# FOX squares summed over heads in two one-pass products of their high and low parts

## What is computed

```python
def rmsnorm(x, g):
    y = xf * lax.rsqrt(jnp.mean(xf * xf, axis=-1, keepdims=True) + NORM_EPS)
    return (y * g)

proj = h @ w_in                                  # q, k, v, gate: 1024 columns each; f: 16
q = rmsnorm(q.reshape(B, L, 16, 64), q_gain) * (64 ** -0.5)
k = rmsnorm(k.reshape(B, L, 16, 64), k_gain)
log_f = jax.nn.log_sigmoid(f + b_f)
c = jnp.cumsum(log_f, axis=1)                    # enters the scores as c_q - c_k
s = q . k + bias, masked;  o = softmax(s) @ v    # per head
out = (o * sigmoid(gate)) @ w_out
```

## Time and profile before

| what | value |
|---|---|
| median of three runs | 2375.32 us (2367.93 to 2377.53) |
| the profiled execution's own time | 2374.61 us |
| its span, first to last instruction | 2373.0 us |
| mean granted TensorE clock | 0.985 |
| busy: TensorE, VectorE, ScalarE, GpSimd | 95%, 66%, 50%, 26% |
| weights and inputs read | 340 MB, 144 GB/s over the span |

### The profile page before, as it was taken

The page is one execution under the profiler, slowest core; times in us unless marked ns, Lnnn a source line. Parts: engine busy times, 40 slices in busy tenths (PEclk is TensorE's granted clock), DMA queues, the critical chain, the costliest instruction groups (busy, mean ns, idle before and its releaser), DMA issues.

```text
span 2373.0 us, 48140 instructions
## 1 busy us (share of the span) xinstructions
PE 2251.4 (95%) x19050; PEld 2141.5 (90%) x19050; DVE 1555.9 (66%) x2516; ACT 1189.3 (50%) x1848; POOL 615.3 (26%) x741
## 2 busy tenths in 40 slices
PE   5999999899999999899999999997999998899998
PEld 4889999899999788799998899997889998798998
DVE  5666554656555676565566665657768976767994
ACT  4555544445544652454445555444556544456553
POOL 4114211004111030031121142217135535033540
PEclk9999999999999998899999999999999999999999
DMA  4224545324546321145453245564354554343554
GB/s 190 89 90 160 177 155 184 123 89 161 177 153 196 114 73 55 54 164 175 161 175 107 89 159 181 171 202 147 110 187 158 180 170 167 103 135 127 188 168 134
DMA packets 52862, 344.02 MB, mean 145 GB/s; under 512 B 5904, under 2 KB 7120, under 8 KB 20176
## 3 DMA queue, kind: packets, MB, share of 16 engines
q1 hardware_dynamic: 51984, 336.26, 42.7%
q0 software_dynamic: 704, 5.31, 0.6%
HBM read 340.43 MB, written 1.05 MB: 144 GB/s over the span
## 4 chain that ended last, share of the span: by engine, by line
PE 73%; DVE 11%; ACT 7%; issue 5%; POOL 2%; DMA 1%; DVEq 0%; ACTq 0%; POOLq 0%
PE ps L767 72%; ACT ring_hi L1497 3%; DVE ring_lo L2037 3%; ACT arena L1497 2%; POOL arena L2938 1%; PE ps L959 1%; DVE newt L2059 1%; DVE arena L2151 1%; DVE newt L2053 1%; DVE hrs L2060 1%; ACT hrs L1497 0%; DMA ring<-in 0%; ACT sq L1497 0%; DMA ring<-out 0%; POOL arena_r L2939 0%
## 5 line engine op out<-in xcount | busy, mean ns | idle before, releaser
L767 PE MATMUL ps<-arena_r,ring_hi 128*128 128x272 f32 (+1 forms) x6688 | 1584.9, 286 | 7.5 <-DVE arena_r L2550 3.2
L767 PEld LDWEIGHTS ps<-arena_r,ring_hi 128*128 128x128 f32 x6688 | 1160.3, 190 | 15.6 <-issue 8.6
L767 PE MATMUL ps<-y_r,ring_hi 128*128 128x272 f32 (+1 forms) x3424 | 1008.8, 295 | 42.0 <-DVE ring_lo L2037 23.7
L2037 DVE TENSOR_TENSOR ring_lo<-ring,ring_hi 128x2048 fp32r<-128x2048 f32 (+2 forms) x372 | 740.5, 1992 | 378.8 <-ACT ring_hi L1497 378.0
L767 PE MATMUL ps<-y_r,ring_lo 128*128 128x272 f32 (+1 forms) x3424 | 978.3, 286 | 0.0
L767 PEld LDWEIGHTS ps<-y_r,ring_hi 128*128 128x128 f32 x3424 | 650.6, 190 | 66.2 <-issue 36.2
L1497 ACT ACTIVATE ring_hi<-ring 128x2048 fp32r<-128x2048 f32 (+2 forms) x372 | 611.4, 1647 | 111.1 <-DMA ring<-dn 52.0
L767 PEld LDWEIGHTS ps<-y_r,ring_lo 128*128 128x128 f32 x3424 | 652.7, 191 | 0.0
L767 PE MATMUL ps<-arena_r,ring_lo 128*128 128x256 f32 (+1 forms) x1632 | 463.9, 284 | 0.0
L767 PEld LDWEIGHTS ps<-arena_r,ring_lo 128*128 128x128 f32 x1632 | 307.9, 189 | 0.0
L1497 ACT ACTIVATE arena<-arena 128x272 f32<-128x272 f32 (+7 forms) x197 | 91.3, 466 | 395.6 <-DVE arena L2620 262.5
(11 more groups left out here) (233 smaller groups left out, 1688.1 us busy)
## 6 DMA issues: line engine op xcount, KB each, us to landing
ring<-gu SPq DMA_DIRECT2D x88, 1024.0 KB, 5.0
ring<-dn SPq DMA_DIRECT2D x64, 704.0 KB, 4.0
ring<-up SPq DMA_DIRECT2D x44, 1024.0 KB, 5.1
ring<-fox_in SPq DMA_DIRECT2D x32, 1024.0 KB, 5.0
ring<-sdn SPq DMA_DIRECT2D x32, 704.0 KB, 4.0
ring<-gdn_in SPq DMA_DIRECT2D x16, 1024.0 KB, 5.0
ring<-in SPq DMA_DIRECT2D x16, 1024.0 KB, 5.1
ring<-gla_in SPq DMA_DIRECT2D x12, 1024.0 KB, 5.1
```

Of the source, the lines that this page charges most:

```text
L767: return nc.tensor.matmul(dst, w, mv, start=start, stop=stop)
L2037: V.tensor_tensor(ring_lo[:, slot, cols], ring[:, slot, cols], ring_hi[:, slot, cols].bitcast(F32), ALU.subtract).then_inc(lo_ready, 2 if ...
```

## The change

The sum over heads no longer multiplies the squares in full precision. ScalarE squares raw twice: once into a rounded tile (f_sq_hi, two tiles in a part of the arena that the late output parts use only later) and once into sq as before. GpSimd subtracts the rounded square from the full one (sq_lo, which lies on sq's own memory). TensorE multiplies halves_r, a rounded copy of halves that ScalarE makes once at the first tile, with f_sq_hi and then with sq_lo, both in one pass, and adds them up in bank 7. ScalarE now signals GpSimd (squared), and GpSimd signals TensorE (hsq_ready). Both FOX stages are changed, 16 query and key tiles in each. The sums of squares in the other stages stay as they are.

```diff
--- before.py
+++ after.py
@@ -300,6 +300,8 @@
         sw_lo = rounded_twin(sw, "sw_lo", 8 * P)
         sw_hi = ctx.enter_context(nc.sbuf_tensor("sw_hi", [P, P], F32R))
         sq = sb("sq", 2, T)
+        sq_lo = rounded_twin(sq, "sq_lo", 2, T)
+        halves_r = ctx.enter_context(nc.sbuf_tensor("halves_r", [P, P], F32R))
         sqsum = sb("sqsum", T)
         rstd = sb("rstd", T)
         mem_rstd = sb("mem_rstd", SEQ)
@@ -373,6 +375,7 @@
         silu_ready = sem("silu_ready")
         h_ready = sem("h_ready")
         hsq_ready = sem("hsq_ready")
+        squared = sem("squared")
         hstat_ready = sem("hstat_ready")
         hrs_ready = sem("hrs_ready")
         stat_taken = sem("stat_taken")
@@ -536,6 +539,7 @@
         xs = x[:, :, META:T]
 
         f_hi_r, f_o_r = view_r(8704, KC, T), view_r(13056, KC, T)
+        f_sq_hi = view_r(8704 + 6 * T, 2, T)
         g_hi_r, g_out_r = view_r(2176, KC, T), view_r(14416, KC, T)
         n_hi_r, n_o_r = view_r(0, KC, T), view_r(16 * T, KC, T)
         h1_r, h1_lo_r = view_r(0, FC, T), view_r(7104, FC, T)
@@ -941,7 +945,8 @@
                         pe.wait_ge(stat_taken, i)
                     elif c:
                         pe.wait_ge(vtok_ready, n.vtok + c)
-                    mm(ps[:, 7, 0:T], halves, sq[:, i % 2, 0:T]).then_inc(hstat_ready, 1)
+                    mm(ps[:, 7, 0:T], halves_r[:, :], f_sq_hi[:, i % 2, :], True, False)
+                    mm(ps[:, 7, 0:T], halves_r[:, :], sq_lo[:, i % 2, :], False, True).then_inc(hstat_ready, 1)
 
                 def values_to_tokens(c):
                     pe.wait_ge(evacuated, BANKS + first_tile + 3 * c + 3)
@@ -1644,12 +1649,16 @@
                             take_turned(u)
                         if FOX_TILES[t - 2][0] == "v":
                             take_tokens(FOX_TILES[t - 2][1])
+                    if t == 0 and j == 0:
+                        fn(halves_r[:, :], halves, ACT.Copy).then_inc(squared, 1)
                     if t == 1:
                         log_sigmoid()
                     if part in "qk":
                         act.wait_ge(evacuated, BANKS + n.tile + t + 1)
                         i = n.head + 2 * c + (part == "k")
-                        fn(sq[:, i % 2, 0:T], raw[:, (2 * c + (part == "k")) % 3, :], ACT.Square).then_inc(hsq_ready, 1)
+                        src = raw[:, (2 * c + (part == "k")) % 3, :]
+                        fn(f_sq_hi[:, i % 2, :], src, ACT.Square).then_inc(squared, 1)
+                        fn(sq[:, i % 2, 0:T], src, ACT.Square).then_inc(squared, 1)
                     if t != 30:
                         before(t)
                     for u in in_slot(units, t):
@@ -2840,10 +2849,16 @@
                 pool.dma_start(qh[FD:FD + 1, :, :], f_rows[0:FH, 5, :]).then_inc(crow_ready, 16)
                 pool.dma_start(kh[FD + 1:FD + 2, :, :], f_rows[0:FH, 4, :]).then_inc(crow_ready, 16)
                 units = fox_units(j)
-                for u, un in enumerate(units):
-                    p = un["p"][0:un["qn"], 0:un["kn"]]
-                    pool.wait_ge(inv_ready, n.inv + u + 1)
-                    G.tensor_scalar(p, p, row_inv[0:un["qn"], u % 4:u % 4 + 1], 1.0, ALU.mult, ALU.mult).then_inc(p_ready, 1)
+                for t, (part, c) in enumerate(FOX_TILES):
+                    for u in in_slot(units, t - 1):
+                        un = units[u]
+                        p = un["p"][0:un["qn"], 0:un["kn"]]
+                        pool.wait_ge(inv_ready, n.inv + u + 1)
+                        G.tensor_scalar(p, p, row_inv[0:un["qn"], u % 4:u % 4 + 1], 1.0, ALU.mult, ALU.mult).then_inc(p_ready, 1)
+                    if part in "qk":
+                        i = 2 * c + (part == "k")
+                        pool.wait_ge(squared, 1 + 2 * (16 * j + i + 1))
+                        G.tensor_tensor(sq_lo[:, i % 2, :], sq[:, i % 2, :], f_sq_hi[:, i % 2, :].bitcast(F32), ALU.subtract).then_inc(hsq_ready, 1)
                 n.inv += len(units)
 
             def gla(tiles):
```

## The result

The changed kernel took 2395.86 us, median of 5 runs (2390.75 to 2402.29), against 2368.09 for the kernel before, median of 5 (2367.45 to 2377.53): ratio 1.0103, 95% interval 1.0078 to 1.0127. A second set of runs beside 29 of the kernel before (median 2367.98) gave 2392.5 and 1.0107 (1.0088 to 1.0127). So by the two ratios, which are taken over all timed runs and are not the quotients of the medians, the change costs about 25 us, 1.05% of 2368. The profiled execution after took 2395.86 with a span of 2394.2, 21.2 more than the profiled one before.

What follows compares the result with a forecast made beforehand. Bound: in FOX stages the ScalarE-VectorE chain often sets the pace despite TensorE's 95%. Terms 9.9 + 3.9 + 4.0 + 0.7 - 1.0 = +17.5 us on 2374.6 gave 2392.1, forecast 2392, range 2382 to 2400.

Steps and rivals of the forecast that it cites:

- the likeliest case: Whole kernel: slower by more than about 0.5% (11.9 us), chance 0.74, against same 0.24 and faster 0.02.
- The start: Start of both FOX stages: first product waits for a GpSimd subtraction behind two DMAs, 7.0 us late; +9.9 us in sum.
- +3.9 for the clock: Tiles 2 and 3 of each FOX stage run at half clock after TensorE's idle time, 1.95 us per stage.
- The second squares: ScalarE's extra squares, 0.33 us each: +4.0 at 12 weight splits, +0.7 at two layer 3 key tiles.
- The saving on TensorE: One-pass pairs for 32 full-precision products save 0.21 us each, 6.7 in all; five counted as really saved, -1.0 us.
- the first rival: FOX stages behind the start: TensorE sets the pace, all savings count, squares cost nothing; +3.2 us, 2377.8; chance 0.15.
- clock term: Start of both FOX stages: half clock behind TensorE's idle time, +3.9 us, bounds 0 and 2 x 3.5.
- GpSimd behind the start: GpSimd's 32 subtractions of 0.76 to 0.85 us: hidden behind the start; up to 1.3 us each if not.
- TensorE sets the pace: FOX stages behind the start: chain has slack, all 32 savings count (-6.7), squares free; +3.2 us, 2377.8; chance 0.15.
- the clock stays up: Start of both FOX stages: no half clock behind the wait, so +13.6 us, 2388.2; chance 0.2.
- the start costs more: GpSimd held after its DMAs or half clock longer, and 28 squares on the chain: +27 us, 2401.7; chance 0.1.
- the signs named: FOX stages: 7 us TensorE wait, equal VectorE idle, half clock, first stage 8 to 9 us longer, 0.3 per weight split.

Runs made afterwards that it cites:

- e2: The changed kernel with 50 one-pass products that nobody reads ahead of each FOX stage's first product, keeping TensorE busy in its wait: 2391.08 us, 1.0083.
- e4: The kernel before with a second, rounded square on ScalarE that nobody reads, ahead of each query or key square: 2377.84 us, 1.0028.
- e5: The kernel before with the sum over heads as one one-pass product of rounded squares, no low part, subtraction or second square: 2375.88 us, 1.0028.
- e10: The changed kernel with each stage's first two subtractions ahead of GpSimd's wait and DMAs, and the weight split ahead of both squares: 2352.89 us, 0.9923.
- e1: The changed kernel with GpSimd's first two subtractions of each FOX stage ahead of its forget-sum wait and two DMAs: 2386.18 us, 1.0069.
- e3: The kernel before with only the wait: GpSimd hands each stage's first two squares to TensorE behind its DMAs: 2385.29 us, 1.0056.
- e6: The changed kernel with one square on ScalarE; GpSimd rounds and subtracts, each stage's first two ahead of its forget-sum wait: 2376.07 us, 1.0027.
- e7: The kernel before with an unread second square on ScalarE, placed behind its tile's weight split and exponentials: 2372.91 us, 1.0024.
- e8: The kernel before with ScalarE's split of the next weights moved ahead of the wait for the tile and its square: 2356.05 us, 0.9937.
- e9: The changed kernel with one square, GpSimd rounding and subtracting (first two early), and the weight split ahead of the square: 2360.75 us, 0.9959.

## Why the prediction was right, and where it was not

The time, 2395.86, lies in the range and is 3.9 above the forecast; the ratio says slower by over 0.5%, the likeliest case. The mechanism was the forecast one, but the terms were not all the right size, and one was missing.

- **The base.** The sum was made against the profiled execution of 2374.6, while the medians of before with more runs are 2368 to 2370. So the cost is near 25 us by the ratios, and 21.2 between the two profiles, not 17.5. A sum too small and a base too high met at 2392; that the time comes so near is in part luck. Of 2368 the 17.5 are 0.74%, so the forecast of slower does not hang on it.
- **The start, +9.9 and +3.9 for the clock.** The first product was forecast at 43.35 and came at 43.19; the start as a whole at 7.05 and 6.75, measured 7.6 and 6.9. e2 splits it: 5.1 and 4.9 without the half clock (5.1 and 4.8 forecast), 2.5 and 2.0 with it (1.95 each). The Trainium skill ("TensorE: Matmul & The Clock Gate", section "Why this matters for your kernels") states that a gap of idle TensorE brings the lower clock back; the trace after agrees, with 0.53 behind 6.85 us of idle time, and e2 shows that filling the gap keeps 1.00.
- **The second squares, +4.0 and +0.7.** The total is right by luck, since two errors cancel. The step took the six weight splits of each stage behind the start, and two of three key tiles without a split in layer 3 alone. e4 shows nine lasting steps of 0.32 in each stage, 5.8 us: the key tiles without a split count in both layers, since the reciprocals of their rows stand on the same chain. But the prediction won nothing back, and the first stage does. Without the clock e4 loses 1.8 and 2.9 us behind the start, 4.7 in all, which is the forecast's figure.
- **The saving on TensorE, -1.0.** Of 6.7 possible I counted five products. e5 shows -0.9 and 0.0 for a saving that is larger by half for each product, so this term was, if anything, too large, and against the first rival it was the right reading. It is a property of the queue on ScalarE, as e10 shows, where more of it counts.
- **What was missing.** The prediction's clock term covered the start alone. Behind the start each stage after has 3.4 us more at half the clock than before: in the first 10.2 in place of 6.8, most of it from 144.4 to 151.3, in the second 1294.7 to 1298.2 with no counterpart. The busy time of both stretches:

```profile
144.40:151.20 6.80, 6.79 (x34) 6.01 (x35) 3.02 (x11) 4.22 (x10) 1.49 (x3) 0.50 0.27 111
1294.70:1298.10 3.40, 3.40 (x18) 3.32 (x16) 0.49 (x2) 1.59 (x6) 0.77 (x1) 0.51 0.42 176
```

Such a stretch costs about 1.5 us: in the second stage the delay against before rises by 1.55 there, and e4 and e5 gave 1.42 to 1.53. The terms then make 7.6 + 1.8 + 1.5 = 10.9 in the first stage, measured 10.5, and 6.9 + 2.9 + 1.5 = 11.3 in the second, measured 11.4; the rest, -0.4 and +0.1, is what is left for the saving, and no larger than the uncertainty of the sum. Where these falls come from is not shown. They don't go with the long wait at the start: e2, whose start has no half clock, has as many as after, and so has e5 with no wait at all, e1 has more, and e3, with a wait of 5.3 us, has none more than before, like e4, e6 and e7. Each of them comes right behind a stretch in which TensorE stood idle in part (before 144.4 it worked for 1.93 of 3.50 us, before 1294.7 for 2.34), but e4 has such stretches too, up to 70.1, 104.2 and 138.3, and no fall behind any of them.

- **GpSimd behind the start** was forecast as hidden. It is: the subtraction ends no wait of TensorE but the first of each stage, and its 32 instructions take 752 to 780 ns.
- **The rivals.** "TensorE sets the pace" falls by e5 and e8, "the clock stays up" by the rows after, "the start costs more" too: the subtraction began at 42.38, 0.07 after the DMA's end. Of the signs named, two came out off: the first FOX stage grew by 10.5 and not 8 to 9, and VectorE's idle time before its first Newton step was 4.6 us and not 7. What the prediction didn't ask is what else stood ahead of the split on ScalarE. Its own view named the wait, 15 us a stage, and only the added square was priced there, not the one that was there already.

## What to carry over

When an instruction is moved into the queue of another engine, look first for the longest wait ahead of it in that queue, at the first tile and not at the steady ones: here 15 of 16 in a stage ended no wait, and one cost 7 us and the clock. When a busy engine still shows short waits every few tiles, don't speed it up; find what the engine behind those waits has in its queue ahead of the step that is waited for, and change the order there (e8: four lines, 15 us). Price a step on such a chain by every place where it stands, and compare stages by the same instruction in both traces, since the whole span moves with the clock.

## What the chip showed that was not expected

**GpSimd and VectorE hold each other up.** A subtraction of 128x272 on GpSimd takes 0.76 us alone, and 2.89 (e1, e10) when it begins with VectorE's 2.27 us weight split; in e10, where the split comes earlier, seven more in each stage behind the start take 1.96 to 2.32. A copy takes 0.41 alone and 2.56 with the split (e6). It goes the other way too. In all kernels GpSimd clears rows of memory ahead of its wait, and VectorE's small operation of 16x272 waits beside it. VectorE and GpSimd in order of time, of before:

```profile
33.98 2.62 DVE L2140 TENSOR_SCALAR arena<-arena,par 16x272 f32<-16x272 f32 x1
...
32.73 3.73 POOL L2838 MEMSET arena<- 2x4352 f32 x1
```

It ends at 36.60 and the clearing at 36.46, while the same form takes 0.29 in the earlier trace rows. In e9 the same instruction begins later, at 35.83, takes 0.77 us and ends at 36.60 too, so it lasts as long as the clearing does. The Trainium skill ("GPSIMD Engine Reference", section "8. Key points") states that GpSimd shares its interfaces to SBUF with VectorE, and that it contends with VectorE instructions that have two inputs in SBUF or run in a 2-port mode. The subtractions agree, with 2.1 us lost to one weight split, which has two such inputs. The 2.62 us instruction has one tile as its input, so by that page it would have to run in a 2-port mode; no run here shows whether it does.

**A half clock while TensorE is busy.** In the profile before, the clock is 0.66 over 68 to 73 us with TensorE busy for all of the 5.00 us, and e4 with nearly the same work there has 1.00. Just before the fall TensorE had stood idle in part, as the first row shows:

```profile
65.00:68.50 3.50, 2.18 (x18) 1.15 (x18) 2.82 (x9) 2.21 (x11) 0.45 (x2) 1.00 0.74 236
68.00:73.00 5.00, 5.00 (x30) 4.83 (x29) 2.65 (x7) 3.13 (x7) 0.77 (x2) 0.66 0.22 93
```

That alone doesn't decide it: in e4 TensorE worked for only 1.85 of the same 3.50 us and the clock stayed up, and before the fall at 935.5 it was busy for 3.50 of 3.50. The totals at half the clock in one execution range from 59 us (e8) to 105 (after), and differ by 12 us between the two profiles of the changed kernel. The longest one, 0.50 from 935.5 to 952.6 in before, stands at 943.2 to 960.2 after and in no other profile of the study at that length. What decides it no run here shows; it is why a difference of 2 or 3 us between two kernels is left open.
